# The last attention's scores: high and low query rows stacked in one 128-row matmul over doubled keys, in place of three passes of half-row pairs

## What is computed

```python
def neighbourhood_attention(q, k, v, rel_bias, rows):
    ...
    scale = HEAD_DIM ** -0.5
    ...
        s = jnp.einsum('bchd,bacwhd->bhcaw', q_r, k_win, preferred_element_type=jnp.float32) * scale
        s = s + bias.transpose(0, 2, 1, 3)[None].astype(jnp.float32)
        p = jax.nn.softmax(s.reshape(bsz, h, GRID_W, kh * kw), axis=-1)
        p = p.reshape(s.shape).astype(v.dtype)
        return jnp.einsum('bhcaw,bacwhd->bchd', p, v_win)
```

## Time and profile before

| | |
|---|---|
| median of 3 runs | 2500.23 us (2499.02 to 2500.62) |
| the profiled execution | 2499.82 us |
| its span in the profile | 2497.6 us |
| mean granted TensorE clock | 0.996 of full |
| busy: PE, PEld | 2438.6 us (98%), 1976.9 us (79%) |
| busy: DVE, ACT, POOL | 1101.5 us (44%), 668.8 us (27%), 1639.5 us (66%) |
| DMA queues | 29.4% of 16 engines on SP's, 1.5% on ScalarE's |

### The profile page before, as it was taken

How to read it: one execution, slowest core, us unless ns; L and a number is a source line. 1 busy time by engine, 2 the same in 40 slices (tenths; PEclk the granted TensorE clock), 3 DMA queues, 4 the chain that set the end, 5 groups by cost and what they waited for, 6 DMA issues and landing times.

```text
span 2497.6 us, 32448 instructions
## 1 busy us (share of the span) xinstructions
PE 2438.6 (98%) x11606; PEld 1976.9 (79%) x11606; DVE 1101.5 (44%) x1465; ACT 668.8 (27%) x1252; POOL 1639.5 (66%) x1431
## 2 busy tenths in 40 slices
PE   7999999999999999999999999999999999999998
PEld 4886678888888887778888888888888787788886
DVE  4454654454333227865333223333226666433311
ACT  4264521112111106652111101111112774211100
POOL 3554856666666776546666776667777775666775
PEclk9999999999999999999999999999999999999999
DMA  6314533233232332003232332333333222232332
GB/s 267 114 59 145 173 114 98 95 96 98 92 101 92 104 107 87 28 13 109 92 101 92 101 109 94 100 93 100 101 104 110 80 74 65 85 100 93 101 101 84
DMA packets 68802, 248.03 MB, mean 99 GB/s; under 512 B 7408, under 2 KB 9968, under 8 KB 68080
## 3 DMA queue, kind: packets, MB, share of 16 engines
q1 hardware_dynamic: 63808, 232.81, 29.4%
q10 hardware_dynamic: 4912, 14.12, 1.5%
HBM read 244.80 MB, written 2.10 MB: 99 GB/s over the span
## 4 chain that ended last, share of the span: by engine, by line
PE 92%; DVE 3%; ACT 2%; issue 1%; POOL 1%; DMA 1%; DVEq 0%; ACTq 0%; POOLq 0%
PE pb L541 72%; PE pb L1098 4%; PE pb L1038 2%; PE pb L806 2%; PE pb L962 2%; PE pb L550 1%; PE pb L740 1%; PE pb L709 1%; PE pb L1081 1%; PE pb L1066 1%; PE pb L1054 1%; PE pb L944 1%; ACT tb L1345 1%; PE pb L928 1%; PE pb L691 1%
## 5 line engine op out<-in xcount | busy, mean ns | idle before, releaser
L541 PE MATMUL pb<-ar,w_hi 128*128 128x512 f32 x5312 | 1644.8, 391 | 3.6 <-DVE ar L1911 2.7
L541 PEld LDWEIGHTS pb<-ar,w_hi 128*128 128x128 f32 x5312 | 995.1, 188 | 222.1 <-issue 8.1
L541 PE MATMUL pb<-ar,w_lo 128*128 128x512 f32 x2656 | 1034.2, 389 | 0.0
L394 POOL TENSOR_TENSOR w_lo<-raw,w_hi 128x1024 fp32r<-128x1024 f32 x380 | 952.1, 2505 | 31.7
L541 PEld LDWEIGHTS pb<-ar,w_lo 128*128 128x128 f32 x2656 | 499.0, 188 | 103.9
L391 POOL TENSOR_TENSOR still<-still 128x1 f32<-128x1 f32 x393 | 81.3, 207 | 693.4 <-PE pb L541 550.8
L392 POOL TENSOR_SCALAR w_hi<-raw 128x1024 fp32r<-128x1024 f32 x380 | 403.7, 1062 | 0.0
L1986 DVE TENSOR_TENSOR tb<-pb,nb 128x512 f32<-128x512 f32 x88 | 60.9, 692 | 400.8 <-PE pb L541 400.8
L1992 DVE TENSOR_TENSOR ar<-tb,ar 128x512 f32 x88 | 156.2, 1775 | 90.9 <-ACT ar L1416 90.9
L1416 ACT ACTIVATE ar<-tb 128x512 f32 x88 | 55.7, 633 | 512.8 <-DVE tb L1989 512.8
L1893 DVE SCALAR_TENSOR_TENSOR x<-pb,x 128x512 f32<-128x512 f32 x48 | 36.2, 755 | 344.2 <-PE pb L541 339.8
(11 more groups left out here) (257 smaller groups left out, 2396.9 us busy)
## 6 DMA issues: line engine op xcount, KB each, us to landing
raw<-wstream SPq DMA_DIRECT2D x428, 512.0 KB, 3.6
raw<-wstream SPq DMA_DIRECT2D x4, 1024.0 KB, 10.7
x<-xt ACTq DMA_DIRECT2D x2, 2048.0 KB, 9.8
tb<-wstream SPq DMA_DIRECT2D x2, 1024.0 KB, 11.7
rt<-wstream SPq DMA_DIRECT2D x2, 1024.0 KB, 11.9
out<-x ACTq DMA_DIRECT2D x8, 256.0 KB, 2.2
rt<-nbias ACTq DMA_DIRECT2D x4, 384.0 KB, 3.8
nb<-nbias ACTq DMA_DIRECT2D x4, 384.0 KB, 3.6
```

The lines of the kernel that those rows point to most:

```text
L394: pool.tensor_tensor(lo, src, hi.bitcast(F32), ALU.subtract).then_inc(s_split, 1)
L541: mm = pe.matmul(pb[:, bank, :], weights(a, n, t)[:, k * P:(k + 1) * P], rhs(b, k0 + k), start=(first and k == 0 and i == 0), stop=(last a ...
```

## The change

The six half-row matmuls of a window become four. The queries of a side now fill all 128 rows of a tile of their own, `O_Q[b][side]`: the high part on the side's own 64 partitions, the low part on the other 64. The high keys exist once for each side, `O_KHI[b][side]`, with the side's 64 rows doubled onto the other 64 partitions. So one full-row matmul for each side gives (query high + query low) by key high. The low keys `O_KLO[b]` stay one tile on 128 partitions; query high by key low is a half-row matmul for each side, and these two stand one after the other as before.

ScalarE's copy of 128x512 becomes two of 64x512, one for each side. VectorE's subtraction becomes two of 64x512; those of the queries write onto the other half of the partitions. For the keys, ScalarE waits for its own two copies and then issues two DMAs on its queue, 64 partitions by 2 KB each, from SBUF to SBUF, which double the rows. TensorE waits for both (`s_kd`) ahead of the first window of each head pair. The second side's high keys use the columns from 29696 on.

```diff
-        O_QK = [[[area(2048 * b + 1024 * w + 512 * s, 1, TOK)[:, 0, :] for s in range(2)]
-                 for w in range(2)] for b in range(2)]
+        O_Q = [[area(2048 * b + 512 * side, 1, TOK)[:, 0, :] for side in range(2)] for b in range(2)]
+        O_KLO = [area(2048 * b + 1024, 1, TOK)[:, 0, :] for b in range(2)]
+        O_KHI = [[area((2048 * b + 1536, 29696 + 512 * b)[side], 1, TOK)[:, 0, :] for side in range(2)] for b in range(2)]
+        HALF_ROWS = (slice(0, 64), slice(64, 128))
...
+        s_kd = [sem(f"keys_doubled{b}") for b in range(2)]
...
-                qq, kk = O_QK[hp % 2]
-                for i, (a, b) in enumerate(PASSES):
-                    for side in range(2):
-                        rows = slice(64 * side, 64 * side + 64)
-                        mm = pe.matmul(pb[:, C_BANKS[side], 0:(hi - lo) * P], qq[a][rows, j * P:(j + 1) * P],
-                                       kk[b][rows, lo * P:hi * P], start=(i == 0), stop=(i == 2))
-                        if i == 2:
-                            mm.then_inc(ct["s"], 1)
+                b, qs, ks = hp % 2, slice(j * P, (j + 1) * P), slice(lo * P, hi * P)
+                if j == 0:
+                    pe.wait_ge(s_kd[b], 32 * (hp // 2 + 1))
+                for side in range(2):
+                    pe.matmul(pb[:, C_BANKS[side], 0:(hi - lo) * P], O_Q[b][side][:, qs], O_KHI[b][side][:, ks],
+                              start=True, stop=False)
+                for side, rows in enumerate(HALF_ROWS):
+                    pe.matmul(pb[:, C_BANKS[side], 0:(hi - lo) * P], O_Q[b][side][rows, qs], O_KLO[b][rows, ks],
+                              start=False, stop=True).then_inc(ct["s"], 1)
...
-                act.activation(O_QK[i % 2][w][0], pb[:, m % 2, :], ACT.Copy, scale=-SCALE if w == 0 else 1.0)\
-                    .then_inc(ct["qk_hi"], 1)
+                hi = (O_Q, O_KHI)[w][i % 2]
+                for side, rows in enumerate(HALF_ROWS):
+                    act.activation(hi[side][rows, :], pb[rows, m % 2, :], ACT.Copy, scale=-SCALE if w == 0 else 1.0)\
+                        .then_inc(ct["qk_hi"], 1)
+                if w == 1:
+                    act.wait_ge(ct["qk_hi"], 2 * m + 2)
+                    for side in range(2):
+                        act.dma_start(hi[side][HALF_ROWS[1 - side], :].bitcast(F32), hi[side][HALF_ROWS[side], :].bitcast(F32))\
+                            .then_inc(s_kd[i % 2], 16)
...
-                dve.wait_ge(ct["qk_hi"], m + 1)
-                dve.scalar_tensor_tensor(O_QK[i % 2][w][1], pb[:, m % 2, :], -SCALE if w == 0 else 1.0,
-                                         O_QK[i % 2][w][0].bitcast(F32), ALU.mult, ALU.subtract)\
-                    .then_inc(s_ev, 1)
+                hi = (O_Q, O_KHI)[w][i % 2]
+                for side, rows in enumerate(HALF_ROWS):
+                    dst = O_KLO[i % 2][rows, :] if w == 1 else O_Q[i % 2][side][HALF_ROWS[1 - side], :]
+                    dve.wait_ge(ct["qk_hi"], 2 * m + side + 1)
+                    ins = dve.scalar_tensor_tensor(dst, pb[rows, m % 2, :], -SCALE if w == 0 else 1.0,
+                                                   hi[side][rows, :].bitcast(F32), ALU.mult, ALU.subtract)
+                ins.then_inc(s_ev, 1)
```

## The result

The changed kernel takes 2510.99 us (median of 5 runs, 2506.29 to 2511.82), the kernel before 2500.53 us (5 runs, 2499.02 to 2501.9). The ratio of their runs is 1.0037, with a 95% interval of 1.0026 to 1.0048: slower by some 10 us. It was wrong.

A forecast was written before the change was run, and what follows sets the result against it. TensorE was taken to bound windows 0 to 26, then a ScalarE, VectorE, TensorE chain. Terms 0.1 + 0.85 = +0.95 us took the profiled 2499.8 to 2500.8, stated as 2501.2 for the median; range 2497.8 to 2506.0.

The forecast's parts named there:

- TensorE's part: Score matmuls in each window: three slots either way, 0.87 us before and after, no gain; +0.1 us over 32 windows for rounding.
- Rival 1: Scores: the lone pair's weights load while full-row matmuls stream, 3.2 us less, 2498.0 us; chance 0.13.
- rival 2: Scores: both full-row weight loads are exposed in every window, 6.4 us more, 2507.6 us; chance 0.07.
- The new wait of TensorE: Before each head pair's first scores, windows 0 to 24: doubled keys land in time after 2.8 us; cost 0, below 0.5 at worst.
- the slack: Time from the second doubling issue to the scores needing it: 5.06 us in the typical window.
- rival 3: Every head pair: doubled-key wait or ScalarE's queue holds TensorE; 2520 us for 7 us transfers, 2505 for 0.8 us issues; chance 0.08.
- The issues: Two doubling DMA issues on ScalarE's queue in key windows, taken to hold it 0.37 us each.
- ScalarE's lateness: Key windows: the next scaling of probabilities starts 1.85 us after the first copy instead of 0.48, so 1.37 us late.
- cover and slack: Typical key window: ScalarE's 1.28 us idle time takes all but 0.1 us, y's low part has 0.49 us spare; TensorE cost 0.
- The last key window: Past window 26, gaps gone: ScalarE's exponential and y's low part come late, +0.85 us once, bounds 0 and 1.4.
- hidden by the wait for y that follows: Last key window: doubled keys landing near 2061.9 against scores at 2061.46 cost nothing extra.
- a wait at the scores that names a DMA: Sign at TensorE's scores that would show the forecast wrong in favour of rival 3.

The follow-up runs named there:

- run 1: The changed kernel with each head pair's keys projected ahead of its queries, so key copy and doubling DMAs come two windows earlier: 2503.08 us, ratio 1.0001 to before.
- run 10: The changed kernel's products with keys projected ahead of queries and the doubling DMAs issued at the end of ScalarE's round: 2500.58 us, ratio 1.0002 to the kernel before.
- run 2: The changed kernel without the doubling DMAs; ScalarE doubles the key rows itself with two more 64x512 copies: 2504.52 us, ratio 1.0014 to the kernel before.
- run 7: The changed kernel with SP holding each weight load next to a key doubling until the doubled keys have landed: 2506.1 us, ratio 1.002 to the kernel before.
- run 4: The kernel before, old products and whole copies, plus the two doubling DMAs into unused columns, without TensorE waiting for them: 2503.09 us, ratio 1.0005.
- run 5: The changed kernel itself, measured again: 2508.9 us, ratio 1.0031 to the kernel before.
- run 9: Keys ahead of queries, four full-row matmuls a window (low keys zero-padded), doublings issued at the end of ScalarE's round: 2499.67 us, ratio 0.9998 to the kernel before.
- run 8: The changed kernel with keys ahead of queries and four full-row matmuls a window, low keys in zero-padded tiles: 2500.98 us, ratio 1.0001 to the kernel before.
- run 3: The kernel before, old products and whole copies, plus the two doubling DMAs into unused columns and TensorE's wait for them: 2504.72 us, ratio 1.0012.
- run 6: The changed kernel with eight matmuls whose result nobody reads filling TensorE's wait in windows 4 and 28: 2506.18 us, ratio 1.0023 to the kernel before.

## Why the prediction was wrong, point by point

- **TensorE's part was right.** Window 11 of the changed kernel, in narrow stretches of TensorE's timeline, against the earlier trace rows:

```profile
1989.68 0.39 PE L1102 MATMUL pb<-ar,w_lo 128*128 128x512 f32 x1
1989.91 0.28 PE L1057 MATMUL pb<-ar 128*128 128x256 f32 x1
...
1990.02 0.28 PE L1057 MATMUL pb<-ar 128*128 128x256 f32 x1
1990.23 0.38 PE L1060 MATMUL pb<-ar 64*128 64x256 f32 x2
...
1990.55 0.33 PE L1070 MATMUL pb<-mat,tb 128*128 128x128 f32 x1
```

  The steps are 0.23, 0.11, 0.21 and 0.32 (forecast 0.23, 0.12, 0.21, 0.31), in sum 0.87 as forecast. Three slots before, three after, and the drain is moved. Rival 1 is out. Of rival 2 there is a trace of 0.08 us in the windows whose first scores wait for keys, and nothing elsewhere. Runs 1 and 10 show the same over the whole stage.
- **The step that failed is "The new wait of TensorE".** I took 2.8 us for a transfer, between rows at 2.2 and 3.8, and 3.8 as the far bound. It measured 4.2 to 5.5 in seven head pairs and 2.3 in the first. The steps into the windows that waited grew by 7.6 us; I had 0. The bias loads that I took 3.8 us from are issued 1.5 to 2.3 us after a weight load, and the doublings of the changed kernel 0.1 to 0.8. I did not look at what SP issues at the time of the key copy, though the trace of the kernel before holds it, for the copy at 1962.17:

```profile
1963.25 0.33 SPq L345 DMA_DIRECT2D raw<-wstream  x1
```

  From the second head pair on, SP issues a weight load 0.93 to 1.15 us after the start of every key copy there, and the working put the first new issue at 1.12. Two bias loads at 1918.04 and 1918.48, 0.5 and 1.0 us behind a weight load, landed after 4.3 and 4.8 us. The transfer by itself was not the error: with nothing ahead of it it takes 2.2 to 2.4 us, less than the 2.8 I took. A second error is in the slack: in the sum I worked it out for the typical window (5.06 us) and for the first head pair, and left out window 4, which only rival 3 counts as worse. The windows ahead of it are short, so that from the key copy to its scores there are 5.26 us (1944.37 to 1949.63 in the kernel before) instead of 6.55, and it was the worst of the first seven, +2.06.
- **The issues were undersized.** 0.50 and 0.67 us from start to start instead of 0.37 each, and the half copies stand 0.60 us apart, not 0.48. ScalarE's lateness of 1.37 us became 1.9 (the scaling starts 2.39 us after the first copy, 1968.15 to 1970.54, against 0.48 before), past cover and slack: where the wait for keys is short or absent (windows 12 and 20), TensorE waits 0.25 to 0.28 us for y, and in runs 2 and 7 in every window from 8 to 24 that follows a key copy, 1.45 and 2.4 us in sum. I had 0.
- **The last key window** was undersized too. Run 4's +0.86 for a forecast of +0.85 is luck: it lacks the half copy that the forecast has in it, and its second issue held the queue 0.85 us. With the half copies, from the start of window 27 to the values matmul that waits for y in window 28 it takes 6.26 us in the kernel before, 7.71 in run 2 and 7.73 in run 7: 1.45 more, 0.1 of it from the new order of the products (6.38 in run 10). In the changed kernel the wait for keys covers this. I had it the other way round, the late keys "hidden by the wait for y that follows", which holds only when the transfer is fast, as in run 7 (0.3 us of wait for keys, then 2.24 for y).
- **The clock was not in the sum at all.** Waits of TensorE of 1.9 to 2.8 us came with 3.4 or 6.8 us at 0.50. Against a step without a fall, 3.4 us at 0.50 cost 1.6 us (6.46 for 4.89 in run 5, 6.52 in run 9 for 4.96 in run 8), and 6.8 us cost some 2.8 (runs 2 and 7, two steps, the longer wait for y taken off). In window 4 a transfer that came 2 us too late cost nearly 4.
- **Rival 3** named this mechanism, a transfer that holds TensorE in every head pair, at 2520 us for 7 us and at 2505 for slow issues, with 0.08. The sign that the prediction gave for it, a wait at the scores that names a DMA, is what the profile shows. It deserved far more: its only counter-evidence, "no transfer of this stage above 3.8 us", takes a median of the earlier trace rows for the longest (one of the four landed after 4.2 us in the kernel before, issued at 1947.01), and none of those was of this kind.

Shown: that the products cost nothing (runs 1 and 10); that the collision with the weight stream makes the transfers slow (runs 3, 4 and 7); and that two things behind the key copy make the loss together, the late landing and ScalarE's hold. They overlap and do not add up: with fast transfers and the hold the stage is still 6.5 us longer than before (run 7), with slow transfers and a shorter hold 4.9 (run 3), without either 0.4 (run 10). Inside ScalarE's hold, the half copies and the issues were not taken apart in one and the same kernel. That the falls of the clock cost 2 to 3 us of the changed kernel's loss rests on steps compared between single profiles and, for run 6, on medians whose intervals overlap. Not tried: the doubling issued from another engine's queue, and the clock's fall by itself in an otherwise equal kernel.

## What to carry to other kernels

When a change puts a DMA between two engines, its price is the landing time in that spot, not the median of its size elsewhere: look up what other queues issue within a few tenths of a microsecond of it, and count the slack in every window, the short ones first. Place such a DMA behind the engine's own urgent work and one stage ahead of its reader; the doublings that cost 10 us here cost under 1 us two windows earlier. Removing the wait that ends last is not enough either: look at what waits behind it, as y did here. And a full-row matmul over zeros can be cheaper than a half-row pair between full-row matmuls, but only while TensorE is what the stage waits for.

## What the runs showed of the hardware

- 128 KB from 64 partitions to the other 64 landed 2.2 to 2.4 us after the issue where the nearest 512 KB weight load of the other queue had been issued 2.1 us or more before (head pair 0 of every run, most pairs of runs 9 and 10) or was held back (run 7, but for one pair at 2.6 and 3.0). It took 3.0 to 4.0 us with a weight load 1.1 to 1.7 us before it (one pair each in runs 8, 9 and 10), 4.0 to 5.8 us with one between 0.8 us before and 0.2 us behind it, and 2.2 to 4.0 us with one 0.3 to 0.8 us behind it (runs 1, 3, 4 and 8).
- A DMA issue behind a semaphore wait held ScalarE's queue 0.47 to 0.53 us and the next one right behind it mostly 0.62, but 0.85 to 1.38 in 12 of 80 pairs, nine of them in runs 3 and 4; a lone issue in the stage took 0.38.
- In the stage, waits of TensorE of 1.90 and 2.44 us (the changed kernel), 2.82 (run 5), 2.72 (run 2), 2.29 (run 3) and 2.24 us (run 7) came with its clock at 0.50 for 3.4 or 6.8 us, which began between 0.7 us before the end of the wait and 1.1 us after it. Waits of 1.57 (run 5), 1.52 (run 1) and 2.26 us (run 4) did not. Two waits 1.4 us apart, 0.89 and 1.44 us, were followed by a fall in run 9; 1.34 and 1.43 us in the same place in run 8 were not. So the length of the wait alone does not tell.
- Switching between full-row and half-row matmuls cost, read from the steps between starts, 0.10 us of drain each way and 0.10 us of weights; in both orders a 256-column window's scores took 0.87 us. Four full-row matmuls instead made a window 0.23 us shorter (256 columns) and 0.16 (384) than either (runs 8 and 9). As the Trainium skill says ("TensorEngine Tiling (Array Packing)", Key Properties), changing the tiling mode drains TensorE.
- VectorE's copies of the low keys, 64x512 fp32r from SBUF to SBUF, took from 0.41 to 1.94 us, median 0.77, in run 9.
